# Keeping the last experts' rows in SBUF in the closing stage of a one-core mixture-of-experts step

## The reference, cut to what matters

```python
sh1, sc1, g1, sh2, sc2, g2 = split(silu(c) @ w_ada + b_ada, 6)   # one row for the prompt, one per request
x = layer_norm(ALPHA * x + (1 + g1) * (merged @ w_o), ln1_g, ln1_b)
h2 = x * (1 + sc2) + sh2
x = layer_norm(ALPHA * x + (1 + g2) * moe(h2), ln2_g, ln2_b)

def moe(h):                      # 16 experts, each token goes to its best 2 of one group of 4
    gate = weights of the two chosen experts, zero elsewhere
    y = zeros_like(h)
    for e in range(16):
        he = silu(h @ w_e_gate[e]) * (h @ w_e_up[e])     # 1024 -> 512
        y = y + gate[..., e:e + 1] * (he @ w_e_down[e])  # 512 -> 1024
    return y
```

## Time and profile before

| | value |
|---|---|
| median of 3 runs | 1103.73 us (1097.69 to 1103.95) |
| profiled execution, its own time | 1103.72 us |
| span of its trace, first to last instruction | 1101.7 us |
| mean granted TensorE clock | 0.952 of full speed |
| TensorE busy / VectorE / GpSimd / ScalarE | 1004.7 / 488.5 / 247.5 / 189.6 us |
| moved by DMA | 214.23 MB |

### The profile page before, as it was taken

The page is one execution under the profiler, slowest core; times in us unless marked ns, Lnnn a source line. Parts: engine busy times, 40 slices in busy tenths (PEclk is TensorE's granted clock), DMA queues, the critical chain, the costliest instruction groups (busy, mean ns, idle before and its releaser), DMA issues. The chain is left out here.

```text
span 1101.7 us, 22153 instructions
## 1 busy us (share of the span) xinstructions
PE 1004.7 (91%) x8966; PEld 672.6 (61%) x8966; DVE 488.5 (44%) x1277; ACT 189.6 (17%) x447; POOL 247.5 (22%) x281
## 2 busy tenths in 40 slices
PE   4999999999899999999999999987999999998940
PEld 3777778456676667677777764565555555555520
DVE  1122999972357788855104005677133011110117
ACT  1110112113121213221111110111111111111103
POOL 0000004536121123222335410000221221111133
PEclk8998999999898999999999999977999999999975
DMA  9964645442514206114081317143969899999856
GB/s 293 306 124 144 196 154 173 175 159 100 212 29 153 64 29 194 31 45 115 11 199 49 115 48 306 67 181 111 354 254 414 332 375 393 419 404 423 349 151 127
DMA packets 93732, 214.23 MB, mean 194 GB/s; under 512 B 23464, under 2 KB 48303, under 8 KB 89533
## 3 DMA queue, kind: packets, MB, share of 16 engines
q1 hardware_dynamic: 78388, 186.20, 47.4%
q0 software_dynamic: 6400, 19.01, 5.8%
q10 hardware_dynamic: 8849, 7.64, 2.6%
HBM read 200.46 MB, written 16.92 MB: 197 GB/s over the span
## 5 line engine op out<-in xcount | busy, mean ns | idle before, releaser
L1765 PE MATMUL bank<-arena 128*128 128x288 f32 (+6 forms) x1778 | 443.0, 405 | 5.4 <-issue 2.1
L1765 PEld LDWEIGHTS bank<-arena 128*128 128x128 f32 (+2 forms) x1778 | 320.8, 192 | 119.5 <-issue 44.7
L2156 PE MATMUL bank<-arena 128*32 128x256 f32 x3136 | 180.6, 381 | 9.2 <-issue 7.1
L2156 PEld LDWEIGHTS bank<-arena 128*32 128x32 f32 x3136 | 102.7, 109 | 79.1 <-issue 12.3
L1717 DVE TENSOR_TENSOR arena<-arena,bank 128x128 f32<-128x128 f32 x49 | 14.2, 289 | 230.7 <-ACT arena L1154 230.5
L917 POOL DMA_INDIRECT expert_rows<-arena,ints x49 | 47.7, 974 | 228.6 <-ACT arena L1165 228.6
L2175 PE MATMUL bank<-arena 128*32 128x256 f32 x1568 | 95.8, 385 | 0.0
L867 POOL TENSOR_SCALAR arena<-arena 128x288 f32<-128x288 f32 x46 | 43.2, 938 | 209.2 <-ACT arena L1107 209.2
L1227 DVE SCALAR_TENSOR_TENSOR arena<-arena 128x512 f32<-128x512 f32 x120 | 81.9, 741 | 0.0
L1779 PE MATMUL bank<-arena 128*128 128x288 f32 x256 | 69.0, 427 | 2.6 <-DVEq L1245 2.6
L1769 PE MATMUL bank<-arena 128*128 128x128 f32 (+7 forms) x315 | 51.2, 297 | 17.3 <-DMA arena<-constants 5.3
(11 more groups left out here) (284 smaller groups left out, 891.4 us busy)
## 6 DMA issues: line engine op xcount, KB each, us to landing
arena<-in_w_e_gate SPq DMA_DIRECT2D x16, 2048.0 KB, 11.9
arena<-in_w_e_up SPq DMA_DIRECT2D x16, 2048.0 KB, 17.1
arena<-in_w_e_down SPq DMA_DIRECT2D x16, 2048.0 KB, 22.2
arena<-in_w_ada SPq DMA_DIRECT2D x8, 2048.0 KB, 10.3
arena<-in_w_in SPq DMA_DIRECT2D x8, 2048.0 KB, 10.0
arena<-in_w_ada SPq DMA_DIRECT2D x8, 1024.0 KB, 11.6
arena<-in_x_prompt SPq DMA_DIRECT2D x8, 512.0 KB, 7.3
arena<-in_w_in SPq DMA_DIRECT2D x14, 256.0 KB, 8.3
```

The source lines that it names most:

```text
L1765: last = pe.matmul(out, a, b, start=k == 0, stop=k == len(pairs_) - 1)
L2156: last = pe.matmul(out, HG[:, g % 2, k, a:a + BLK], gate_up[i % 2][:, :, k, c * P:c * P + P], start=k == 0, stop=k == KT - 1)
```

## The change

It does five things.

1. The last five blocks (`KEPT = 5`, blocks 44 to 48) are no longer scattered. Their rows stay in SBUF. After the loop TensorE adds them into each token tile by products with one-hot matrices (`kept_hot`), which VectorE builds in blocks 21 to 25. In each product 32 rows of a block quarter are contracted to 128 tokens, 256 columns wide; there are 20 products per token tile, and their four quarters go to four PSUM banks.
2. GpSimd scatters zeros to the DRAM places of those five blocks (`kept_rows`, issued with blocks 24 to 28), so that the areas can be added as a whole.
3. The multiplication by the gate row moves from the closing stage into the loop. For every block GpSimd gathers the gate quarters from DRAM (`gate_rows`, 128 x 1 KB, two blocks ahead), and VectorE, in place of ScalarE, evacuates the down product times the token's weight times the gate (`result_up`). The two gate-row loads of turn 9 go.
4. SP's loads of the rows go. GpSimd adds both areas into `X1` by accumulating DMAs: five for the first area in one go, then five for the second, each after the tile's first. They start when blocks 0 to 43 are stored.
5. In the plan `lnA2` and `lnA1` go ahead of `mix` and `ada 11`.

```diff
+SENT = FIRST[NE - 2]
+KEPT = NBLK - SENT
@@ make_plan
-    plan += [("lnA1", 2), ("lnA2", 1), ("nat", "u", 4), ("mix", 0), ("ada", 11), ("lnA1", 3), ("lnA2", 2), ("mix", 1), ("mix", 2), ("lnA1", 4), ("lnA2", 3)]
-    plan += [("yc", 0), ("mix", 3), ("lnA2", 4), ("yc", 1), ("yc", 2)]
+    plan += [("lnA1", 2), ("lnA2", 1), ("nat", "u", 4), ("lnA2", 2), ("lnA1", 3), ("mix", 0), ("ada", 11), ("lnA1", 4), ("lnA2", 3), ("mix", 1), ("mix", 2)]
+    plan += [("lnA2", 4), ("yc", 0), ("mix", 3), ("yc", 1), ("yc", 2)]
@@ SP
-                sp.dma_start(BC2[:, 0, :], mod_d[0:1, 5 * D:6 * D].partition_broadcast(P)).then_inc(ev("rows2_in"), 16)
-                sp.dma_start(BC2[0:NS, 1, :], bass.AP(mod_d.tensor, ...)).then_inc(ev("rows2_in"), 16)
...
-        for t in range(NT):
-            sp.dma_start(GAT[0:rows_of(t), t, :], y_d[t * P:t * P + rows_of(t), :]).then_inc(ev(f"tile_in{t}"), 16)
@@ GpSimd
+        def gate_rows(d):
+            ready = ev(f"g2_in{d % 2}" if d < SENT else "g2_in")
+            pool.indirect_dma_start(G2B[gates_of(d)], None, gates, bass.IndirectOffsetOnAxis(ints[:, I_ROW + d:I_ROW + d + 1], 0)).then_inc(ready, 16)
+        def kept_rows(k):
+            c = SENT + k
+            gate_rows(c)
+            pool.indirect_dma_start(quarters, bass.IndirectOffsetOnAxis(ints[:, I_DEST + c:I_DEST + c + 1], 0), ZERO[:, 0:256], None).then_inc(ev("g2_in"), 16)
+        def add_rows(t, second, src):
+            a = t * P + SLEN * second
+            pool.dma_start(X1[0:rows_of(t), t, :], src[a:a + rows_of(t), :], accum_op=ALU.add).then_inc(ev(f"pair_in{t}"), 16)
...
+        for d in range(SENT):
             ...
             pool.wait_ge(ev("yo_up"), d + 1)
+            pool.indirect_dma_start(quarters, bass.IndirectOffsetOnAxis(ints[:, I_DEST + d:I_DEST + d + 1], 0), YR[:, yr_of(d), :], None).then_inc(stored(d)[0], 16)
+            if d + 2 < SENT:
+                gate_rows(d + 2)
+            if 24 <= d < 24 + KEPT:
+                kept_rows(d - 24)
...
+        pool.wait_ge(ev("g2_in"), 32 * KEPT)
+        for done_ in stored_by(SENT):
+            pool.wait_ge(*done_)
+        with pool.If(nov > 0):
...
+        for t in range(NT):
+            add_rows(t, 0, y_d)
+        for t in range(NT):
+            pool.wait_ge(ev(f"pair_in{t}"), 16)
+            add_rows(t, 1, y_d)
         for s in range(NOV):
             with pool.If(nov > s):
...
+        for s in range(NOV):
+            with pool.If(nov > s):
+                pool.wait_ge(*far_stored(s // 2 + 1, s % 2))
+        with pool.If(nov > 0):
...
+        pool.sem_inc(ev("further_added"), 1)
@@ ScalarE, expert loop
-                act.activation(YR[:, d % YRS, :], banks[6 + d % 2][:, 0:256], ACT.Copy, scale=WBLK[:, d:d + 1]).then_inc(ev("yo_up"), 1)
@@ VectorE, expert loop
+        def result_up(d):
+            dve.wait_ge(ev("dn_full"), d + 1)
+            ...
+            if d < SENT:
+                dve.wait_ge(ev(f"g2_in{d % 2}"), 16 * (d // 2 + 1))
+            else:
+                dve.wait_ge(ev("g2_in"), 32 * KEPT)
+            stt(YR[:, yr_of(d), :], banks[6 + d % 2][:, 0:256], WBLK[:, d:d + 1], G2B[gates_of(d)], ALU.mult, ALU.mult).then_inc(ev("yo_up"), 1)
+        def kept_hot(k):
+            link(tt_(OHT[k], KOFF[:, k, :].unsqueeze(2).broadcast_to([P, NT, TS]), RCON[:, R_LO:].unsqueeze(1).broadcast_to([P, NT, TS]), ALU.is_equal))
@@ VectorE, closing stage
+        dve.wait_ge(ev("further_added"), 1)
         for t in range(NT):
-            dve.wait_ge(ev(f"pair_in{t}"), 16)
-            link(tt_(a, a, BC2[0:n, 0 if t < 4 else 1, :], ALU.mult))
-            link(dve.tensor_tensor_reduce(out=a, in0=a, in1=X1[0:n, t, :], scale=1.0, scalar=0.0, op0=ALU.add, op1=ALU.add, accum_out=m))
+            dve.wait_ge(ev(f"pair_in{t}"), 32)
+            dve.wait_ge(ev("rows_summed"), t + 1)
+            link(dve.tensor_tensor_reduce(out=by_quarter, in0=by_quarter, in1=sums[0:n], scale=1.0, scalar=0.0, op0=ALU.add, op1=ALU.add, accum_out=total))
@@ TensorE, after the loop
+        for t in range(NT):
+            n = rows_of(t)
+            if t == 1:
+                pe.wait_ge(ev("yo_up"), NBLK)
+            if t >= 2:
+                pe.wait_ge(ev("row_mean"), t - 1)
+            for k in range(KEPT):
+                if t == 0:
+                    pe.wait_ge(ev("yo_up"), SENT + k + 1)
+                for c in range(4):
+                    rows = slice(BLK * c, BLK * c + BLK)
+                    last = pe.matmul(sum_banks(t)[0:n, c, :], OHT[k][rows, t, 0:n], YR[rows, YRS + k, :],
+                                     start=k == 0, stop=k == KEPT - 1)
+            last.then_inc(ev("rows_summed"), 1)
```

More of the change, by code:

```diff
@@ L45 @@
 YRS = 4
+PLACES = 2048
 TURNS = [0, 1, 2, 11, 3, 12, 4, 13, 5, 6, 7, 8, 14, 9, 10, 15]
@@ L769, in _ @@
         each_further(sp, nov, further_weights)
-        sp.wait_ge(ev("hid_full"), FIRST[NE - 1])
-        for done_ in stored_by(FIRST[NE - 1]):
-            sp.wait_ge(*done_)
-        with sp.If(nov > 0):
-            for done_ in stored_by(NBLK):
-                sp.wait_ge(*done_)
-        for s in range(NOV):
-            with sp.If(nov > s):
-                sp.wait_ge(*far_stored(s // 2 + 1, s % 2))
-        for t in range(NT):
-            sp.dma_start(GAT[0:rows_of(t), t, :], y_d[t * P:t * P + rows_of(t), :]).then_inc(ev(f"tile_in{t}"), 16)
         for t in (3, 4):
@@ L907, in _ @@
         quarters = y_d.rearrange("r (c f) -> (r c) f", c=4)
-        for d in range(NBLK):
-            if d == 0:
-                pool.wait_ge(ev("weights_up"), 1)
+        gates = mod_d.rearrange("r (k f) -> (r k) f", f=256)
+        def gate_rows(d):
[8 more added lines that the diff above has]
+            pool.dma_start(X1[0:rows_of(t), t, :], src[a:a + rows_of(t), :], accum_op=ALU.add).then_inc(ev(f"pair_in{t}"), 16)
+        own.link(pool.memset(ZERO, 0.0))
+        pool.wait_ge(ev("weights_up"), 1)
+        gate_rows(0)
+        gate_rows(1)
+        for d in range(SENT):
             for g in range(2, TILES):
@@ L996, in _ @@
                 for g in range(4):
-                    last = act.activation(mod_buf(n)[:, g * P:g * P + P], mm.tile(key)[32 * g:32 * g + 9, 0:P], ACT.Copy)
+                    last = act.activation(mod_buf(n)[:, g * P:g * P + P], mm.tile(key)[32 * g:32 * g + 9, 0:P], ACT.Copy, bias=1.0 if n >= 10 else 0.0)
                     own.done(last) if g < 3 else last.then_inc(mm.free(key), 1)
@@ L1150, in _ @@
         act.activation(HG[:, 0, 4:8, :], quarter_tiles(banks[4]), ACT.Copy).then_inc(ev("gt_b"), 1)
-        for b in range(NBLK + 2):
-            if b < NBLK:
-                act.wait_ge(ev("hid_full"), b + 1)
-                act.activation(HEB[:, b % 3, :], banks[b % 3][:, 0:P], ACT.Silu).then_inc(ev("he_silu"), 1)
+        for b in range(NBLK):
+            act.wait_ge(ev("hid_full"), b + 1)
+            act.activation(HEB[:, b % 3, :], banks[b % 3][:, 0:P], ACT.Silu).then_inc(ev("he_silu"), 1)
             if b in tile_behind:
@@ L1734, in _ @@
                 spread_up()
+            if b >= 3:
+                if b == 3:
+                    result_up(0)
+                result_up(b - 2)
         nov = dve.value_load(ints[0:1, I_NOV:I_NOV + 1], min_val=0, max_val=NOV)
@@ L2222, in _ @@
         each_further(pe, nov, further)
+        with pe.If(nov > 0):
+            pe.wait_ge(ev("further_added"), 1)
+        pe.wait_ge(ev("he_ready"), NBLK)
+        pe.wait_ge(ev("het_up"), NBLK)
+        for t in range(NT):
+            n = rows_of(t)
+            if t == 1:
[10 more added lines that the diff above has]
+            last.then_inc(ev("rows_summed"), 1)
 def buckets():
@@ L2252, in constants @@
     c[:, K_STEP:K_STEP + NOV] = np.arange(NOV)[None, :]
-    c[:, K_DEST:K_DEST + 2 * NT] = p + P * np.arange(2 * NT)[None, :] + 1
+    token = p + P * np.arange(NT)[None, :]
+    row = np.where((token >= SEQ) & (token < NTOK), (token - SEQ) // ST + 1, 0)
+    c[:, K_DEST:K_DEST + 2 * NT] = p + P * np.arange(2 * NT)[None, :] + 1 + PLACES * np.concatenate([row, row], 1)
+    c[:, K_ROW:K_ROW + 1] = 12 + p // BLK
+    c[:, K_CND:K_CND + NB] = PLACES * np.arange(1, NB + 1)[None, :]
     c[:, K_LEFT:K_LEFT + 1] = p + 2 * SLEN + 1
```

163 lines of the change are left out of this document (98 added, 65 removed).

## The result

The changed kernel takes 1106.7 us (median of 20 runs, 1101.11 to 1112.2), the kernel before beside it 1103.18 (20 runs, 1095.44 to 1106.9). The ratio is 1.0045 with a 95% interval of 1.0028 to 1.0063: half a per cent slower, where 1097 and a small gain were forecast. The changed kernel's profiled execution took 1105.81 us, with a span of 1103.7.

The account below looks back on a forecast made before the run. In the expert loop TensorE and the weight stream were taken as both close to full, DMA engines 98.7% busy. Terms -2.2 + 7 - 11.6 = -6.8 us on 1103.72 gave 1097 us; range 1085 to 1108.

Parts of the forecast that it names:

- Front part, -2.2: Before the expert loop: reordered plan removes the 4.30 us stand, gate product then waits for its weight; gain between 0 and 4.9.
- Expert loop, +7: Expert loop: gate rows and zeros lengthen it by 7 us on full DMA engines; bounds 0 and +10.
- The bytes, +7: Expert loop: 35 transfers at 0.34 us of all engines, 11.8 together; less credits 5.8, plus 1.0 at the early stall.
- The sign that was to come with them: Expert loop: if right, waits for weights grow to some 15 us.
- the sum's 5.8: Expert loop: 11.8 us of transfers, less 1.9 for dropped gate-row loads, 2.2 free engine time and 1.9 slack.
- the credits taken off: Expert loop: 2.2 us for the engines' free 1.3% and 1.9 us slack between last up load and its product.
- The early stall, +1.0: Expert loop: the weight stall at 863 us is lengthened by some three fetches, 1.0 us.
- VectorE's eviction and the one-hot rows: Expert loop: about 0.42 us per block, one-hot builds one wide operation in five blocks; hidden in the 6.13 us block.
- The rival that the gate fetch paces the loop: Expert loop: mean landing above 9.9 us makes gate fetches set the pace; at 11 us, 1120 us in all; chance 0.10.
- the rival of free fetches: Expert loop: engines sustain 426 GB/s, so the +7 is 0 and the time 1090 us; chance 0.22.
- Closing stage, -11.6: After the loop: adds wait for block 43's scatter, begun some 20 us earlier, VectorE released at 1065.0; bounds -16 and -6.
- The rival of quarters in series: Closing stage: TensorE's array quarters run serially, 8.7 us a tile of sums, 1121 us in all; chance 0.06.

Follow-up runs that it names:

- burst: Kernel before plus 15 unused indirect transfers of 128 1 KB rows, three behind each scatter of blocks 24 to 28; 1112.44 us, ratio 1.0099.
- paced: Changed kernel with the same transfers spread in time: gate fetches and gathers held back, kept rows' ten transfers one each behind ten blocks; 1101.91 us, ratio 1.0007.
- no_gates: Changed kernel with transfers spread in time, without the 49 gate fetches, rows multiplied by one; loop 305.2 us, median 1127.26 us (late in front).
- resident_plain: Changed kernel with prompt gate in SBUF instead of gate fetches, samples gated in a closing tile, zeros one a block; 1088.29 us, ratio 0.9868.

## Why the prediction was wrong

- **Front part, -2.2: right** in its rows. Forecast: the gate product at 285.9 and 8.70 for the group; measured 284.73 and 8.78. That the whole stage came out at -2.7 is partly luck, since profiles with one and the same front part differ by 4.8 us.
- **Expert loop, +7 with a bound of +10: the step that failed**, 17.6 on the trace. The failing sentence is that GpSimd's additional indirect transfers are hidden because their issue takes less than a block. That counted GpSimd's own time alone. Three or more in a row cost TensorE 4.5 us at the start, about 8 us in the five kept blocks, which burst reproduced, and 5.6 at the token gathers. No row of before could show it: there never more than two go out in a row.
- **The bytes, +7: right in price, but they did not show as forecast.** A transfer costs 0.35 us against 0.34. The sign that was to come with them, waits for weights of some 15 us, did not come in the changed kernel (7.6 us at first products, 8.0 before); the gaps stood in its place. Where the gaps are gone, in paced, these waits are 5.7 us longer than before, near the sum's 5.8; but 3.1 us of slow products behind them come on top, which the sum had not counted. With loops that scatter by 2 to 4.5 us the credits taken off (free engine time and slack ahead of the last up load, 4.1 us together) are neither shown nor ruled out. The upper end is given as +10, though its terms (5.8, 2.2 and 1.0) make 9. The early stall, +1.0, did not come: the wait at that place is 1.0 us against 0.8.
- **Hidden: VectorE's eviction and the one-hot rows, right;** no_gates has both, and its loop is 1.9 above before, within the scatter. The gate wait was hidden but for the start, where VectorE waited for gate rows twice ahead of its first results; behind that the first burst went out. The rival that the gate fetch paces the loop fell. So did the rival of free fetches: the mean rate was 398 GB/s with engines as full as before.
- **Closing stage, -11.6: near in size by luck, not in its cause.** VectorE's tile was 2.71 against 2.73. But its start was set by TensorE's idle 5.17 us and a first tile of sums of nearly 5 (1077.64 to 1082.49), not by the additions: 10.0 us behind the last down product instead of the 7.4 forecast. The forecast had the first two tiles summed behind the additions and put the way from loop to sums at nothing. The fifth mean came 22.1 us behind the last down product where it had been 32.65, 10.5 earlier instead of 13.1; the rest, 2.3, is behind that mean, where I had forecast no change (9.1 us instead of 11.4). The rival of quarters in series fell: 2.3 us a tile.

## What to carry to other kernels

Count the indirect transfers that go out in a row, not only their bytes and their issuer's free time: from the third on they cost TensorE's products time here. Spacing them took the gaps away, but not the price of their bytes. On DMA engines that were already full the repeated fetch of a small table was paid in weight stalls; with the table in SBUF and each block's copy made by ScalarE the loop was as long as before. When a stall has two causes, taking one away shows the other: paced alone gave 2.8 us of 17.6.

## What the runs showed of the hardware

- Three or more indirect transfers of 128 rows in a row on GpSimd made groups of TensorE products that wait for nothing falter: with three, 32 products of 1.94 us took 2.5 to 3.0, with four or five up to 5.3, whether the rows were 1 KB or 64 bytes long. Two in a row, or three direct ones behind a scatter, did nothing of the kind.
- Behind its last down product TensorE needed 5.17 us to load a value and jump over the unused work, with no wait in the profile (3.63 in resident_plain). The Trainium skill's section "Instruction fetch mechanics" ("Runtime: NRT & Kernel Launch") says that a jump out of the fetched window waits for a fetch; the packets agree with it. In all five traces with the sums behind the jump (the changed kernel twice, paced, no_gates and resident_plain) one packet of the instruction queue q8 moves in this gap, and the first sum starts 1.8 us behind its end: at 1077.64 behind 1075.83 in the changed kernel, at 1054.06 behind 1052.25 in resident_plain. The changed kernel's queue list from 1072.5 to 1077.6 us:

```profile
q8 instruction: 1, 0.02, 1.2%
```

- After a wait TensorE often began at the half clock level, granted near 0.50: 64 products then took 5.35 us instead of 3.66 (paced, behind a wait of 2.27 us), a tile of sums 4.85 instead of 2.3. Not always: in the kernel before, products behind a wait of 3.58 us ran at 1.00.
